# Expert weights in 2 MB transfers of two ring slots instead of 1 MB transfers of one, in a one-core encoder layer

## The reference, cut to what is computed

```python
h = rmsnorm(x, mix_norm_g); q, k, v, gb, gc, u = split(h @ w_in)
x = x + concat(rmsnorm(attention(q, k, v)), rmsnorm(conv(gb, gc, u))) @ w_out
h = rmsnorm(x, ffn_norm_g)
gates, experts = softmax(top4(h @ w_router + b_router))
# for each expert e, on the tokens that chose it:
hu = h[tok] @ w_gate_up[e] + b_gate_up[e]            # 1024 -> 2048
act = a * sigmoid(1.702 * a) * (lin + 1)             # a, lin: the clamped halves of hu
y[tok] += gate * (act @ w_down[e] + b_down[e])       # 1024 -> 1024
out = rmsnorm(x + y, final_norm_g)
```

## Time and profile before

| | |
|---|---|
| median of three runs | 1372.1 us |
| the profiled execution, its time | 1373.16 us |
| the profiled execution, its span | 1371.3 us |
| TensorE matmul busy | 1317.0 us, 96% of the span |
| TensorE weight load busy (beside the matmuls) | 647.4 us, 47% |
| VectorE, ScalarE, GpSimd busy | 37%, 15%, 19% |
| moved by DMA | 450.79 MB, mean 329 GB/s |
| chain of work that ended last | TensorE 76%, DMA 9%, VectorE 5% |

### The profile page before, as it was taken

One profiled execution on the slowest core, in us unless ns is written; L12 is line 12 of the kernel. 1 busy time (PEld: TensorE's weight loads), 2 busy tenths in 40 slices (PEclk: granted clock), 3 DMA queues, 4 the chain that ended last, 5 costly groups with the idle time before them and its releaser, 6 DMA issues.

```text
span 1371.3 us, 33077 instructions
## 1 busy us (share of the span) xinstructions
PE 1317.0 (96%) x13998; PEld 647.4 (47%) x13998; DVE 504.3 (37%) x884; ACT 205.0 (15%) x313; POOL 267.0 (19%) x258
## 2 busy tenths in 40 slices
PE   6989999988999999999999999999999999999996
PEld 5766676882444444444444444444444434444443
DVE  7456653561233222222333333322222222333335
ACT  5134433230001000000010000100000000110002
POOL 1825427024011111111111111111111111111100
PEclk9999999979999999999999999999999999999998
DMA  9322113566999999999999999999999999999984
GB/s 245 82 62 62 62 62 105 223 236 226 348 398 406 403 408 400 402 410 407 402 403 407 398 402 407 412 407 406 404 406 406 407 408 404 409 408 402 406 354 143
DMA packets 94605, 450.79 MB, mean 329 GB/s; under 512 B 12105, under 2 KB 36953, under 8 KB 45424
## 3 DMA queue, kind: packets, MB, share of 16 engines
q1 hardware_dynamic: 83280, 426.27, 77.7%
q0 software_dynamic: 8656, 19.51, 5.9%
q10 hardware_dynamic: 2640, 4.59, 0.9%
HBM read 440.08 MB, written 18.67 MB: 335 GB/s over the span
## 4 chain that ended last, share of the span: by engine, by line
PE 76%; DMA 9%; DVE 5%; issue 4%; POOL 2%; SPq 2%; ACT 1%; DVEq 0%; POOLq 0%; ACTq 0%
PE gu_bank L1551 40%; PE bank L1565 21%; DMA raw<-in_w_gate_up_dram 9%; PE bank L1316 3%; PE bank L1318 3%; PE bank L1317 3%; PE bank L1539 2%; SPq L385 2%; PE bank L1393 1%; DVE probs_a L1030 1%; PE bank L1407 1%; PE bank L1518 1%; PE bank L1568 1%; DMA x_sb<-in_x_dram 1%; DVE lo L955 1%
## 5 line engine op out<-in xcount | busy, mean ns | idle before, releaser
L1551 PE MATMUL gu_bank<-raw,xT 128*32 128x512 f32 x3072 | 341.2, 593 | 6.0 <-DMA raw<-in_w_gate_up_dram 3.1
L1212 DVE TENSOR_TENSOR gate_in<-gu_bank,b_gu 128x768 f32<-128x768 f32 x32 | 30.6, 958 | 571.1 <-PE gu_bank L1551 538.9
L1551 PEld LDWEIGHTS gu_bank<-raw,xT 128*32 128x32 f32 x3072 | 101.2, 110 | 238.9 <-issue 220.2
L1565 PE MATMUL bank<-raw_a,aT 128*32 128x256 f32 x2232 | 166.8, 380 | 0.0
L1568 PE MATMUL bank<-raw_a,aT 128*32 128x256 f32 x744 | 166.4, 380 | 0.0
L1551 PE MATMUL gu_bank<-raw_c,xT 128*32 128x512 f32 x1488 | 165.5, 592 | 0.0
L586 POOL DMA_INDIRECT sum_rows<-y_out,scatter_list x31 | 45.2, 1457 | 429.7 <-ACT y_out L852 429.7
L1237 DVE STREAM_TRANSPOSE aT<-lin_in 128x192 f32<-128x192 f32 x128 | 67.8, 532 | 143.4 <-PE bank L1568 142.3
L1565 PEld LDWEIGHTS bank<-raw_a,aT 128*32 128x32 f32 x2232 | 88.8, 110 | 62.0
L838 ACT ACTIVATE xT<-bank 128x384 f32<-128x384 f32 x66 | 28.9, 488 | 554.8 <-PE bank L1539 539.6
L1551 PEld LDWEIGHTS gu_bank<-raw_c,xT 128*32 128x32 f32 x1488 | 49.4, 110 | 110.3 <-issue 105.3
(11 more groups left out here) (240 smaller groups left out, 1628.8 us busy)
## 6 DMA issues: line engine op xcount, KB each, us to landing
raw<-in_w_gate_up_dram SPq DMA_DIRECT2D x128, 1024.0 KB
raw_c<-in_w_gate_up_dram SPq DMA_DIRECT2D x62, 1024.0 KB
raw_a<-in_w_down_dram SPq DMA_DIRECT2D x62, 1024.0 KB
raw_b<-in_w_gate_up_dram SPq DMA_DIRECT2D x32, 1024.0 KB
raw_b<-in_w_down_dram SPq DMA_DIRECT2D x32, 1024.0 KB
raw_e<-in_w_gate_up_dram SPq DMA_DIRECT2D x31, 1024.0 KB
raw_d<-in_w_down_dram SPq DMA_DIRECT2D x31, 1024.0 KB
raw<-in_w_in_dram SPq DMA_DIRECT2D x24, 512.0 KB, 5.2
```

The lines of the kernel that those rows point to most:

```text
L1212: dve.tensor_tensor(gate_in[:, :, :], gu_bank[:, :, 0:QUARTER], gate_b, ALU.add)
L1551: ins = pe.matmul(gu_bank[c * GROUP:(c + 1) * GROUP, r, :], xT[:, i, r * GROUP:(r + 1) * GROUP], w[:, c], start=first, stop=last)
L1565: pe.matmul(bank_[c * GROUP:(c + 1) * GROUP, cols], aT[:, k, c * GROUP:(c + 1) * GROUP], w[:, at:at + QUARTER], start=first and r % 2 == 0 ...
```

## The change

Weights are now loaded two chunks at a time, 2 MB in one transfer, into two neighbouring slots. A partition gets one 16 KB run: two neighbouring rows of `w_gate_up` (rows 2p and 2p+1 of a block of 256), or four neighbouring rows of `w_down`. Each chunk is still used by itself, in the same order. The pair has one semaphore, that of its even slot. The load of a pair waits until both chunks that held the slots before are used.

As gate and up chunk i now holds every second row of a 256-row block, the input must be laid out the same way: slice i of `xT` is made from every second column of a block of 256 (`row_of`), both in the transposes and in the product that makes the first `xT`.

Every pair needs two neighbouring slots, so the single slots `raw_d` and `raw_e` are gone, and a new pair `raw_h` lies in the room of `hi01`. The order of slots is now `raw01` (0 to 3), `raw_a` (4, 5), `raw_b` (6, 7), `raw_h` (8, 9), `raw_c` (10, 11). The waits of the first twelve chunks change with that.

```diff
+        with ExitStack() as experts_only:
+            raw_h = experts_only.enter_context(nc.sbuf_tensor("raw_h", [P, 2, CHUNK], F32))
         raw_g = sb("raw_g", [P, 2 * SPLIT_FRONT, CHUNK])
...
-            for ring in (raw01, raw_a, raw_d, raw_b, raw_e, raw_c):
+            for ring in (raw01, raw_a, raw_b, raw_h, raw_c):
...
+        def raw_pair(m):
+            for ring in (raw01, raw_a, raw_b, raw_h, raw_c):
+                if m < ring.shape[1]:
+                    return ring[:, m:m + 2, :]
+                m -= ring.shape[1]
+        def row_of(i):
+            return slice(i // 2 * 2 * P + i % 2, (i // 2 + 1) * 2 * P, 2)
...
-                sp.dma_start(raw_slot(m % RAW), w_gate_up[0, e, i * P:(i + 1) * P, :]).then_inc(w_loaded[m % RAW], 16)
+                sp.dma_start(raw_pair(m % RAW),
+                             w_gate_up[0, e].rearrange("(i p h) n -> i p h n", p=P, h=2)[i // 2])\
+                  .then_inc(w_loaded[m % RAW], 16)
...
-                sp.dma_start(raw_slot(m % RAW),
-                             w_down[0, e].rearrange("(p i h) n -> i p (h n)", p=P, i=DN_CHUNKS)[i])\
+                sp.dma_start(raw_pair(m % RAW),
+                             w_down[0, e].rearrange("(p i h q) n -> i p h (q n)", p=P, i=DN_CHUNKS // 2, h=2)[i // 2])\
...
-                used = fixed(sp, later(m - (RAW - 1), b, BODY * JOB)) if m >= RAW else 0
+                used = fixed(sp, later(m + 1 - (RAW - 1), b, BODY * JOB)) if m >= RAW else 0
                 if m < RAW_FRONT:
-                    s = N_IN + m
+                    s = N_IN + m + 1
...
                 elif m == RAW_FRONT + 2:
-                    sp.wait_ge(lists_emptied, 16)
-                elif m == RAW_FRONT + 3:
                     wait_used(sp, N_FRONT - 1)
-                elif m == RAW_FRONT + 5:
-                    sp.wait_ge(ss_1_ready, TT)
...
-                for i in range(GU_CHUNKS):
+                for i in range(0, GU_CHUNKS, 2):
                     load_gu(e, i, gu_chunk(n, i), b, turns)
-                for i in range(DN_CHUNKS):
+                for i in range(0, DN_CHUNKS, 2):
                     load_dn(before_e, i, dn_chunk(n - 1, i), b, turns)
...
-                    ins = pe.matmul(bank[6 + k // TT][:, (k % TT) * TILE:(k % TT + 1) * TILE], xn[:, t, k * P:(k + 1) * P],
+                    ins = pe.matmul(bank[6 + k // TT][:, (k % TT) * TILE:(k % TT + 1) * TILE], xn[:, t, row_of(k)],
...
-                                           src[0:TILE, (g * TT + k) * P:(g * TT + k + 1) * P],
+                                           src[0:TILE, row_of(g * TT + k)],
...
             def gate_up(m, i, loads):
-                pe.wait_ge(w_loaded[m % RAW], loads)
+                pe.wait_ge(w_loaded[m % RAW // 2 * 2], loads)
...
             def down(m, i, loads, first_bank=4):
-                pe.wait_ge(w_loaded[m % RAW], loads)
+                pe.wait_ge(w_loaded[m % RAW // 2 * 2], loads)
```

More of the change, by code:

```diff
@@ L195, in build @@
             ("sig_in", [P, GROUPS, QUARTER], F32))
[L196 to L200, removed]
+        y_out, raw_c = overlay(64 * K, ("y_out", [P, D_MODEL], F32), ("raw_c", [P, 2, CHUNK], F32))
+        b_dn, b_row, b_gu, raw_a = overlay(98 * K, ("b_dn", [P, 2 * D_FF], F32), ("b_row", [P, 2, QUARTER], F32),
+                                           ("b_gu", [P, 2, QUARTER], F32), ("raw_a", [P, 2, CHUNK], F32))
         g_fin_row = overlay(92 * K, ("g_fin_row", [P, D_MODEL], F32))
```

## The result

The changed kernel takes 1378.1 us (median of 15 runs, 1374.3 to 1379.8) against 1370.7 us for the kernel before (15 runs, 1367.4 to 1375.4). The ratio is 1.0049, 95% interval 1.0038 to 1.0059: about 7 us slower. The forecast was 1368.0 us, some 4 us under the 1372.1 it counted from; the time fell into the upper end of the range and moved the other way.

The account below looks back on a forecast made before the run. TensorE was taken to set the loop's pace, with slightly slower DMA hidden by the ring until late stalls. 1373.2 - 4.8 + 0.7 = 1369.1 us, 1368.0 against the median; range 1363 to 1379, the forecast's own 1366 to 1371.

Parts of the forecast that it names:

- What bounds the kernel: Expert loop: TensorE sets the pace until weight transfers stall it late; DMA gains can give back at most 4.8 us.
- The one pace of 32.71 us for both stretches: Expert loop: DMA needs 32.71 us a job throughout against TensorE's 31.91, so the lead shrinks by 0.81 us a job.
- Transposes from every second column: TensorE's eight transpose weight loads a job, now reading floats 8 bytes apart: taken as nothing, bounds 0 to 22 us.
- The rival: Transposes in TensorE's job: strided weight loads take twice as long, job 32.6 us, total 1390 us; chance 0.06.
- Longer runs: Weight transfers: a 16 KB packet takes 600 ns instead of 620, 3% less, counted as 2% of DMA time.
- the prediction's sum: Loop stalls from starting lead and loss a job: none at 1.0% DMA saving, 5.4 us at 0.5%.
- Coarser ring: Weight ring: pairs issued and usable one chunk later each, 5.4 us of lead lost, leaving 14.2 us at the start.
- All 4.8 us come back: Expert loop: with a loss of 0.18 us a job the lead lasts, so the 4.8 us of stalls vanish.
- The front: Before the first expert: the `sum_rows` store lands 2.3 us later, 1.6 covered, 0.7 us lost; bounds 0 and 2.3.
- Waits and issues: TensorE's semaphore waits, SyncE's load issues, and gathers and scatters in the loop: no cost.
- The range: Total time: 1363 to 1379 us, holding the forecast, little-or-nothing and faster-first-expert cases but their edges.
- the case in which the run pays nothing: Rival on weight transfers: 16 KB runs save little or nothing, stalls start earlier, 1378 us with nothing saved; chance 0.17.

Follow-up runs that it names:

- the second trace of the kernel before: The kernel before, unchanged, profiled again in the second stretch of runs: 1358.8 us in the profiled run, stalls 5.3 us.
- the paired waits: Kernel before with two slots waited for and used together, filled by two 1 MB transfers of 8 KB runs, contiguous transposes: 1363.1 us, ratio 1.0018.
- the contiguous transposes: Changed kernel with columns reordered once where normed tokens meet the gain, so transposes read contiguous slices: 1361.2 us, ratio 0.9998 against the kernel before.
- The layout alone: Kernel before with only the change's row layout and strided transposes, 1 MB transfers, 8 KB runs, old ring: 1366.0 us against 1360.9, ratio 1.0027.

## Why the prediction was wrong, step by step

- **What bounds the kernel**: right in what it was used for. A pair ring with nothing saved has 10.6 us of stalls where 10.3 was worked out, and 4.8 us was the most that DMA could give back. The one pace of 32.71 us for both stretches was too simple. The lead can be read from the landings, as the time from the landing of a job's first load to the start of that job. In the second trace of the kernel before it is 20.6 us at 394 us and 0.3 at 1096, 0.93 us a job instead of 0.81.
- **Transposes from every second column**: the step that failed and turned the sign. It was put at nothing between bounds of 0 and 22 us. It costs 1.13 - 0.81 = 0.32 us a job, 9.9 us over 31 jobs, because the weight load takes 214 to 217 ns instead of 141. The reasoning, that 1.1 ns a column leaves room for a stride of one more float, had no row behind it; the rule of the Trainium skill (SBUF — State Buffer, the note on 16-byte cachelines) agreed with it, and these rows contradict it. The middle of the bounds, 11 us, would have been nearly exact, but by luck: a load is longer by some 75 ns, and the pace of the eight only by 40 ns each (0.32 / 8). The rival named the right place and had twice the price, since it took loads twice as long and all of that on the path. Its chance was 0.06, where the trace gave no reason to prefer zero.
- **Longer runs**: the mechanism was right, the size off. The line through a 4 KB store and an 8 KB load gave 3%, taken as 2%. Weight loads alone in 256:260 us of the changed kernel:

```profile
DMA packets 121, 1.72 MB, mean 430 GB/s; under 512 B 16, under 2 KB 16, under 8 KB 16
...
q1 hardware_dynamic: 121, 1.72, 100.5%
```

  64.3 engine-us for 105 packets are 613 ns each; two of 8 KB take 620. That is 1.2%. The stores of the earlier trace rows had made the 4 KB packet too dear, and the fixed part came out at 20 ns; these two figures give about 7. Under load it is a little less. q1 in 440:840, first with 8 KB runs (the paired waits), then with 16 KB (the contiguous transposes):

```profile
q1 hardware_dynamic: 21210, 154.47, 94.2%
```

```profile
q1 hardware_dynamic: 10638, 154.96, 93.6%
```

  Per byte that is 1.0% less share, with an error of 0.1 in either share. By the prediction's sum one percent would leave no stall and half a percent 5.4 us; 6.2 came, against 10.6 with 8 KB runs in a pair ring. The landings show where the sum went wrong. From 397 to 844 us the lead falls from 15.8 to 4.3 us with 16 KB runs, and with 8 KB runs from 15.9 to 0.5 (395 to 842 us): 0.82 against 1.10 us a job, 0.9% of a job less, as the share has it. Both fall faster than the sum had them. And once the ring is empty nothing is saved: stalled jobs take 32.73 us with either, (1253.46 - 1024.38) / 7 and (1255.92 - 863.21) / 12. Why that is isn't shown. The run is just worth the lead that its pairs cost: 6.2 us of stalls against 5.3 before, ratio 0.9998.
- **Coarser ring**: right, 5.4 us of lead, 5.3 us more stalls (10.6 against 5.3).
- **All 4.8 us come back**: they did, but not by the forecast's reason. The layout alone removes them too, since a slower TensorE drains the ring more slowly: by the landings its lead is 21.7 us at 396 us and still 2.8 at 1299, 0.67 us a job, where the kernel before loses 0.93. A trace without stalls looked like a success of the change and was a by-product of its cost: with the pace of before, the same transfers leave 6.2 us.
- **The front**: 0.7 us was forecast, none is seen. `sum_rows` did land later, 10.6 us after its issue instead of 9.6:

```profile
sum_rows<-x ACTq DMA_DIRECT2D x1, 512.0 KB, 10.6
```

  That is 1.0 us and not 2.3, within the 1.6 us of cover that the step had counted. TensorE's wait for VectorE's scaled tokens ahead of the first `xT` is 2.0 us instead of 0.3 all the same; in the whole of the front, 2.5 us shorter, no cost can be told.
- **Waits and issues**: nothing, as said.
- **The range** was 1363 to 1379. It held the time by luck, since its upper end was there for the case in which the run pays nothing; the case that came true was priced outside it.

## What to carry to other kernels

A change of data layout for the sake of DMA is paid for by every engine that reads the data; where TensorE sets the pace, look for the strided operand first, and put the reordering where it happens once (here at the gain, in the front) or make the change only on data that needs none (here the down weights). When two engines are within 2% of each other, price the change by the lead of the buffer between them: a coarser ring costs its granularity twice, and a stall that vanishes can mean that the consumer slowed down. An unknown with bounds from 0 to 22 us is not a zero.

## What the runs showed of the hardware

- A weight load of 128 float32 columns takes 141 ns contiguous, 217 ns from every second column and 219 ns from every fourth: at these two strides the price is for being strided, not for the distance.
- A 16 KB packet takes 613 ns and two of 8 KB 620 when the weights are alone on the queues.
- A loop body of one or two experts needs 21 to 24 instruction packets in the whole run, one of four experts 120, and then TensorE loses 8.3 us in a pass (jobs of 37.5 and 34.6 us instead of 31.9).
- The same product, the first expert's, takes 20.8 us in most traces (22.0 in one) and 31.6 to 32.3 us in the first two and the last two, the kernel before and the changed one alike, and makes the 10 us between the stretches. The number of the chip doesn't decide it: chip 2 is on record with either time. What holds TensorE there wasn't tested.
